# The second block's attention by pairs of heads, with the context's ahead and the convolution, pooling and output projections between the pairs

## What is computed

```python
h, hc = mod_norm(x, ...), mod_norm(xc, ...)
u = h @ w_in[l]
if last:  # second layer: of the context only keys and values
    kc, vc = heads(uc_kv[..., :NA_CH]), heads(uc_kv[..., NA_CH:])
else:
    yc = concatenate([gated_conv_mixer(...), multiscale_pool_mixer(...),
                      context_attention(heads(uc q), kc, vc)]) @ w_out[l]
    xc = xc + mc[:, 5, None] * yc
    xc = ffn_sublayer(xc, ...)
y = concatenate([gated_conv_mixer(...), multiscale_pool_mixer(...),
                 neighbourhood_attention(q, k, v, kc, vc, rpb[l])]) @ w_out[l]
x = x + m[:, 5, None] * y
```

## Time and profile before

| | us |
|---|---|
| median of 3 runs | 3614.18 (3612.76 to 3615.71) |
| the profiled execution | 3613.57 |
| its span in the profile | 3611.7 |

### The profile page before, as it was taken

One profiled execution on the slowest core, in us unless ns is written; L12 is line 12 of the kernel. 1 busy time (PEld: TensorE's weight loads), 2 busy tenths in 40 slices (PEclk: granted clock), 3 DMA queues, 4 the chain that ended last, 5 costly groups with the idle time before them and its releaser, 6 DMA issues.

```text
span 3611.7 us, 45968 instructions
## 1 busy us (share of the span) xinstructions
PE 3454.8 (96%) x18726; PEld 2954.7 (82%) x18726; DVE 1875.9 (52%) x3704; ACT 1145.2 (32%) x1886; POOL 275.4 (8%) x520
## 2 busy tenths in 40 slices
PE   6989899998999999999989999999999999999998
PEld 5778668886888888978878888888888888878886
DVE  5476678446555526356567774352222364653333
ACT  4465433224221224225432122242112242433222
POOL 0000011000111100301011110000000012100000
PEclk9999899999999999999999999999999999999999
DMA  4201245333434423410345553232122243123332
GB/s 125 91 24 43 74 136 179 99 100 112 130 125 129 118 72 115 123 47 13 94 152 159 158 161 108 85 103 65 59 65 65 76 135 108 33 60 98 94 99 76
DMA packets 381235, 352.57 MB, mean 98 GB/s; under 512 B 19440, under 2 KB 353136, under 8 KB 380640
## 3 DMA queue, kind: packets, MB, share of 16 engines
q1 hardware_dynamic: 348416, 255.47, 23.3%
q0 software_dynamic: 31168, 91.94, 8.4%
q10 hardware_dynamic: 1440, 2.22, 0.2%
HBM read 343.27 MB, written 2.10 MB: 96 GB/s over the span
## 4 chain that ended last, share of the span: by engine, by line
PE 85%; DVE 10%; ACT 4%; issue 1%; DMA 1%; ACTq 0%; DVEq 0%; POOLq 0%
PE ps L536 83%; PE ps L539 2%; DVE lob L1787 2%; DVE Tm L1899 1%; ACT hib L1178 1%; DVE Hl L1910 1%; DVE ACC L1876 1%; ACT Tm L1178 1%; ACT Hh L1178 1%; ACT L1178 0%; DVE HN L1919 0%; DVE MR L1807 0%; DVE Hl L1908 0%; DVE near_PTt L2435 0%; DVE C L1960 0%
## 5 line engine op out<-in xcount | busy, mean ns | idle before, releaser
L536 PE MATMUL ps<-Hh,hib 128*128 128x512 f32 (+1 forms) x3552 | 1260.7, 355 | 26.5 <-DVE lob L1787 16.8
L536 PE MATMUL ps<-Hl,hib 128*128 128x512 f32 (+1 forms) x3552 | 1253.1, 353 | 0.0
L536 PE MATMUL ps<-Hh,lob 128*128 128x512 f32 (+1 forms) x3552 | 1251.0, 352 | 0.0
L1787 DVE TENSOR_TENSOR lob<-rawb,hib 128x1024 fp32r<-128x1024 f32 (+2 forms) x487 | 582.9, 1199 | 1013.1 <-ACT hib L1178 1012.5
L1178 ACT ACTIVATE hib<-rawb 128x1024 fp32r<-128x1024 f32 (+2 forms) x487 | 501.1, 1033 | 1266.2 <-PE ps L536 1242.6
L536 PEld LDWEIGHTS ps<-Hh,hib 128*128 128x128 f32 x3552 | 677.9, 191 | 132.0 <-DVE lob L1787 19.8
L536 PEld LDWEIGHTS ps<-Hh,lob 128*128 128x128 f32 x3552 | 676.8, 191 | 91.1
L536 PEld LDWEIGHTS ps<-Hl,hib 128*128 128x128 f32 x3552 | 678.1, 191 | 89.3 <-issue 1.2
L536 PE MATMUL ps<-Gha,hib 128*128 128x512 f32 (+1 forms) x704 | 239.7, 340 | 6.6 <-DVE lob L1787 6.5
L536 PE MATMUL ps<-Gla,hib 128*128 128x512 f32 (+1 forms) x704 | 238.1, 338 | 0.0
L536 PE MATMUL ps<-Gha,lob 128*128 128x512 f32 (+1 forms) x704 | 238.1, 338 | 0.0
(11 more groups left out here) (254 smaller groups left out, 4018.1 us busy)
## 6 DMA issues: line engine op xcount, KB each, us to landing
rawb<-in_ffn_w_in SPq DMA_DIRECT2D x352, 256.0 KB, 3.3
rawb<-in_ffn_w_out SPq DMA_DIRECT2D x88, 512.0 KB, 3.4
MRb<-in_w_mod_t POOLq DMA_DIRECT2D x144, 256.0 KB, 3.4
rawb<-in_w_ff SPq DMA_DIRECT2D x64, 512.0 KB, 3.6
rawb<-in_w_in SPq DMA_DIRECT2D x62, 512.0 KB, 3.7
MRa<-in_w_mod_t POOLq DMA_DIRECT2D x96, 256.0 KB, 3.4
rawb<-in_ffn_w_out SPq DMA_DIRECT2D x44, 384.0 KB, 3.1
rawb<-in_w_out SPq DMA_DIRECT2D x28, 512.0 KB, 3.4
```

What stands on the lines that cost most here:

```text
L536: return e.matmul(out, lhsT, rhs, start=start, stop=stop)
L1787: e.tensor_tensor(lob_of(c), raw_of(c), hib_of(c), ALU.subtract).then_inc(*done(("lo", c.i)))
```

## The change

The chunks of `v2` have 512 columns. In layer 0 `conv`, `pool` and `q2` are swept for `c` alone first (12 chunks), then the context's attention runs, by pairs of heads (8 pairs), and `pool` and `conv` for `x` are swept tile by tile between those pairs; then the context's output projection, `q2` for `x`, and the attention of `x` (16 pairs) with the first half of its output projection (the four slices of convolution and pooling) between the first pairs. In layer 1 `q2` comes ahead of `conv` and `pool`, which lie between the pairs; the first half of the output projection starts behind the last scores. The queries of `x` go to the columns of `c` in `Hh` and `Hl`, so they need not wait until the sweeps of `x` are done. The second half of the output projection is last; in layer 0 the norm of `c` lies in it, and the norm of `x` lies between the first chunks of sublayer `b`. A pair is two heads of one block: PE makes both heads' scores, transposes and outputs in one step each, in the order transposes of p-2, scores of p, the work beside, outputs of p-2; DVE's order is scores of p, scaling of p-1, the work beside, final of p-3. What is left out of the diff: the same moves written for ACT, and functions of DVE that hold the old code under new names (`conv_stage`, `pooled`, `projected`, `mix_cp`, `half_residual`).

```diff
@@ -283,16 +283,38 @@
         ffn(("a", l), d["ffn_w_in_2"][l, 0], d["ffn_w_out_2"][l, 0], ["x", "c"], True)
         w = d["w_in_2"][l]
         for s, tiles in (("x", 4), ("c", 2)):
-            for half in range(2):
-                tm(("v2", l, s, half), w, 8, 2048 + 256 * half, 256, tiles)
+            tm(("v2", l, s), w, 8, 2048, 512, tiles)
         for pair in range(2):
             fm(("k2", l, pair), w, 8, [1536 + 256 * pair, 1664 + 256 * pair], ["x", "c"])
-        for stage, c0 in enumerate((0, 512, 256)):
-            fm(("conv", l, stage), w, 8, [c0, c0 + 128], full)
-        fm(("pool", l), w, 8, [768, 896], full)
-        for pair in range(2):
-            fm(("q2", l, pair), w, 8, [1024 + 256 * pair, 1152 + 256 * pair], full)
-        residual(("out2", l), d["w_out_2"][l], 8, full, l == 0)
+        def conv(s):
+            for stage, c0 in enumerate((0, 512, 256)):
+                fm(("conv", l, s, stage), w, 8, [c0, c0 + 128], [s])
+        def pool(s):
+            fm(("pool", l, s), w, 8, [768, 896], [s])
+        def queries(s):
+            for pair in range(2):
+                fm(("q2", l, s, pair), w, 8, [1024 + 256 * pair, 1152 + 256 * pair], [s])
+        if l == 0:
+            conv("c")
+            pool("c")
+            queries("c")
+            pool("x")
+            conv("x")
+            residual(("out2", l), d["w_out_2"][l], 8, ["c"], False)
+            queries("x")
+        else:
+            queries("x")
+            conv("x")
+            pool("x")
+        for half in range(2):
+            for pair in range(4):
+                name = (("out2", l, half), "x", pair)
+                P[name] = Sweep(name, [chunk(beside(d["w_out_2"][l][512 * half:512 * half + 512, 256 * pair:256 * pair + 256].rearrange(
+                    "(k p) n -> p k n", p=128)), 4 * half, 4, 256)], [(0, "x"), (1, "x")])
         ffn(("b", l), d["ffn_w_in_2"][l, 1], d["ffn_w_out_2"][l, 1], full, l == 0)
...
+def near_pairs(s):
+    return [(hp, j) for hp in range(4) for j in range(4 if s == "x" else 2)]
...
+def beside_pairs(l, s):
+    at = {n: [] for n in range(30)}
+    def put(step, *what):
+        at[step].append(what)
+    if (l, s) == (0, "c"):
+        put(1, "mix", "c")
+        for q in range(4):
+            put(q // 2, "tile", ("pool", l, "x"))
+            for stage in range(3):
+                put(2 + 2 * stage + q // 2, "tile", ("conv", l, "x", stage))
+        for n in range(2):
+            put(2 + n, "pooled", n)
+            put(4 + n, "project", n)
+            put(5 + n, "projected", n)
+        for stage in range(3):
+            put(4 + 2 * stage, "conv", stage)
+    elif l == 0:
+        put(0, "mix", "x")
+        for pair in range(4):
+            for n in range(2):
+                put(2 * pair + n + 1, "out", pair)
+            put(2 * pair + 3, "added", pair)
+    else:
+        for stage in range(3):
+            for q in range(4):
+                put((4 * stage + q) * 2 // 3, "tile", ("conv", l, "x", stage))
+            put((4 * stage + 3) * 2 // 3 + 1, "conv", stage)
+        for q in range(4):
+            put(8 + q // 2, "tile", ("pool", l, "x"))
+        for n in range(2):
+            put(10 + n, "pooled", n)
+            put(12 + n, "project", n)
+            put(13 + n, "projected", n)
+        put(15, "mix", "x")
+        for n in range(2):
+            put(17 + n, "out", 0)
+    return at
...
+def by_pairs(number, stages, skew, beside, beside_do):
+    for step in range(number + skew[-1]):
+        for f, late in zip(stages, skew):
+            if f == "beside":
+                for what, n in beside.get(step, []):
+                    beside_do(what, n)
+            elif f is not None and 0 <= step - late < number:
+                f(step - late)
...
+        def second_at(H_, k, s, j):
+            return query_at(H_, k, j) if s == "x" else H_[:, 4 + k, T + 128 * j:T + 128 * j + 128]
+        def made_at(H_, l, k, s, j):
+            return H_[:, 4 + k, 128 * j:128 * j + 128] if (l, s) == (0, "x") else second_at(H_, k, s, j)
+        def pool_buffer(l):
+            return near[l]["PTt"] if l == 0 else C[:, :, :].rearrange("p a b -> p (a b)")
+        def turned_keys(l, s, p, b):
+            return near[l]["PTt"][:, 512 * b:512 * b + 512] if s == "x" else near[l]["P"][:, 2 * (p % 2) + b, 256:512]
...
+                def n_scores(p_):
+                    hp, j = pairs[p_]
+                    w.wait_ge(*at("q2", l, s, hp))
...
+                    got = [take("s2", l, s, p_, b) for b in range(2)]
+                    for b, (bank, before) in enumerate(got):
+                        freed(before)
+                        if s == "x":
+                            w.wait_ge(*at("maskr", l))
+                            w.wait_ge(*at("identr"))
+                            mm(ps[:, bank, 0:256], identr[:, :], N["maskr"][:, 256 * KIND[j]:256 * KIND[j] + 256], True, False)
+                    for b in range(2):
+                        r = slice(64 * b, 64 * b + 64)
...
+                        if s == "x":
+                            bank = got[b][0]
+                            scores(ps[:, bank, 0:256].rearrange("p (i c) -> p i c", c=32), q_, near_keys, False)
+                            m = scores(ps[:, bank, 256:512], q_, context_keys, True)
+                        else:
+                            m = scores(ps[:, got[b][0], 0:TC], q_, context_keys, True)
+                    m.then_inc(*done(("scores2", l, s, p_)))
...
+                def n_turn(p_):
+                    n = 4 if s == "x" else 2
+                    got = [take("t2", l, s, p_, b) for b in range(2 if s == "x" else 1)]
+                    w.wait_ge(*at("scaled2", l, s, p_))
+                    for b in range(2):
+                        bank, before = got[b % len(got)]
+                        freed(before)
+                        for k in range(n):
+                            to = 128 * k + (0 if s == "x" else 256 * b)
+                            m = turn(ps[:, bank, to:to + 128], N["P"][:, 2 * (p_ % 2) + b, 128 * k:128 * k + 128])
+                    m.then_inc(*done(("turned2", l, s, p_)))
...
+                outs = [by_tile((("out2", l, 0), "x", pair), fm_products, mixed_acts(l), l == 0) for pair in range(4)]
+                by_pairs(len(pairs), [n_turn, n_scores, "beside", n_out, n_final], [2, 0, 0, 2, 3], beside_pairs(l, s), beside_do)
+                return outs
...
+            def project(l, s, n):
...
+                w.wait_ge(*at("pooled", l, s, n))
+                freed(before)
+                mm(ps[:, b, 0:nt], N["PW"][:, n, :], N["PV"][:, n, t0:t0 + nt], True, True).then_inc(*done(("pwfull", l, s, n)))
...
             def near_mixers(l):
                 acts = {"x": x_act(4 + 3 * l), "c": c_act(2 + 3 * l)}
                 for s in ("x", "c"):
+                    whole(("v2", l, s), tm_products, tm_act(acts[s]), cnorm(l, 1) if s == "x" else None)
+                    give_all(("v2", l, s))
                 for pair in range(2):
                     whole(("k2", l, pair), fm_products, acts)
                     give_all(("k2", l, pair))
+                if l == 0:
+                    for stage in range(3):
+                        whole(("conv", l, "c", stage), fm_products, acts)
+                        give_all(("conv", l, "c", stage))
+                    whole(("pool", l, "c"), fm_products, acts)
+                    give_all(("pool", l, "c"))
+                    for pair in range(2):
+                        whole(("q2", l, "c", pair), fm_products, acts)
+                        give_all(("q2", l, "c", pair))
+                    mark("pe", "hfree", "c", l)
+                    for n in range(2):
+                        project(l, "c", n)
+                        give("pw", l, "c", n)
+                    near_attention(l, "c")
+                    residual(("out2", l), ["c"], {"c": (Hh, Hl, T, TC, (lambda k: ("mix2", l, "c", k)), False)})
+                mark("pe", "cfree", l)
                 for pair in range(2):
+                    whole(("q2", l, "x", pair), fm_products, acts)
+                    give_all(("q2", l, "x", pair))
+                if l == 0:
+                    mark("pe", "hfree", "x", l)
+                outs = near_attention(l, "x")
+                for some in outs:
+                    for _ in some:
+                        pass
+                mark("pe", "qfree", l)
+                if l == 0:
+                    in_turn(grouped(norm_steps(*cnorm(l, 2)), NORM_BY_4))
+                residual(("out2", l, 1), ["x"], mixed_acts(l))
...
+                def n_turn(p_):
+                    w.wait_ge(*at("turned2", l, s, p_))
+                    if p_:
+                        w.wait_ge(*at("pout2", l, s, p_ - 1))
+                    elif s == "x":
+                        w.wait_ge(*at("pooled", 0, "x", 1) if l == 0 else (None, 0))
+                    if s == "x":
+                        for b in range(2):
```

(60 more changed lines are left out.)

598 lines of the change are left out of this document (294 added, 304 removed).

## The result

The change makes the kernel faster, where I forecast no gain: 3591.98 us (median of 4 runs, 3590.48 to 3599.08) against 3614.94 us (4 runs beside them), ratio 0.9939 (95% interval 0.9922 to 0.9957). The forecast was 3622 us, 3600 to 3640: wrong in its sign, and 8 us outside the range.

The account below looks back on a forecast made before the run. PE was taken as the bound. From the profiled 3613.57 us, 44.5 taken away and 47.2 added made +2.7, the clock +5.0: 3621.3, or 3622 us for the median, range 3600 to 3640.

Parts of the forecast that it names:

- The attention's switches: In both layers' attention a pair of x costs PE 4.91 us against 5.28 before; with c's pairs, -15.0 us.
- rival E: Last score of one head and first of the other overlap in all 40 pairs: -5, 3617 us; chance 0.07.
- small: Layer 1's halved slice multiplications +1.2 us, start 0.5, convolution bursts on DVE, banks and 24 switches to tiles 3.0.
- Pairs with nothing beside them: Attention steps without tiles: PE waits 1.3 us a pair for DVE's chain, 6.2 in all; layer 0 +11.0 us.
- Rival A: Pairs without tiles do not wait, DVE's chain taking under 2.3 us: 3601 us; chance 0.20.
- Starts: Start of c's attention: waits 1.8 and 2.3, +5.5 us; of x's in layer 0: waits 2.5 and 2.1, +6.5.
- Layer 1, steps 10 to 15: Two poolings of x on DVE under pairs without tiles: transposes wait 11.9 us, step 15 adds 2.0; +13.9 in all.
- Sweeps for c: Twelve chunks for c alone run at 2.9 us a chunk, cost 0; up to +8 us if loads lag.
- rival C: c's sweeps run at the pace of their loads, 0.7 us late in each of twelve: +8, 3630 us; chance 0.07.
- Layer 0's end: Behind layer 0 PE idles 17.2 us against 14.3, +2.9, and x's halves add 1.9: together +4.8 us.
- The clock: Half clock at pairs without tiles and layer 1's waits of 3.5 and 4.1 us: +5 us (0 to 14).
- rival B: Half clock lasts, three falls of 6 us each: 3632 us; sign: granted clock under 0.8 over tileless pairs; chance 0.15.

Follow-up runs that it names:

- pool_first: Changed kernel with layer 1's pooling sweep ahead of the convolution's, its two poolings in steps 2 and 3: 3589.36 us, ratio 0.9932 to the kernel before.
- heads_alternate: Changed kernel with the two heads' matmuls alternating, score by score and output by output: 3586.05 us, ratio 0.9931 to the kernel before.
- Scale_first: Changed kernel with DVE scaling the weights of pair p-1 before the scores of pair p: 3580.28 us, ratio 0.9912 to the kernel before.
- masks_apart: Changed kernel with each head's mask matmul directly ahead of its own six scores in pairs of x: 3619.26 us, ratio 1.0018 to the kernel before.

## Why the prediction was wrong, point by point

**The step that failed is "The attention's switches", its 4.91 us a pair, and with it rival E, which I priced at one score's 0.12 us.** Measured are 4.03. Not one score but three run beside the other head's, and four outputs do. Of the 0.88, 0.39 lie in the scores (1.25 for 1.64) and some 0.53 in the outputs (1.51 for 2.04). The steps with a tile, some 16 of the 32, save all of it, 14 us. In the others only the scores' part shortens the step, as the chain begins at the last score, and the outputs' part turned into wait (1.66 for my 1.3): the step is 5.75 us for 6.2, which saves 7. A pair of c costs 1.74 (outputs 0.60, transposes 0.58, scores 0.56) and not 2.56: both heads' scores, three each, run wholly side by side, and so do the outputs, four each; that is -6.5. Against it the tiles of a step cost 0.23 more than forecast (one 2.96 for 2.73, two 5.68 for 5.46), in 26 steps 6, of which 3.0 stood under "small": +3. Together -24 or -25 of the 26 us by which the profiled execution, its first part's 3.8 set aside, lies under my 3621.3. The median lies 30 us under my 3622, so some 5 are left; 3.4 of them, an estimate, are what the profiled execution took longer in layer 0 than two others of the same code, mostly by its clock (pool_first above).

**Why misled me.** I took eight outputs in a row in 1.12 us as two heads that don't overlap. They were four and four, and the second four had to wait for a copy on ACT. These are that stretch's weight loads and copy, from the trace of before:

```profile
1726.52 0.41 PEld L536 LDWEIGHTS ps<-near_PTt,near_VX 128*64 128x64 f32 x4 [0.17 <-issue]
...
1727.06 0.41 PEld L536 LDWEIGHTS ps<-near_PTt,near_VX 128*64 128x64 f32 x4
...
1726.62 0.38 ACT L1178 ACTIVATE near_PTt<-ps 128x256 f32<-128x256 f32 x1 [0.56 <-PE ps L539]
```

The copy ends at 1727.00, and the second four begin at 1727.06. The row joined two groups that were never free to overlap. With it I had argued the rival down to 0.07. The Trainium skill ("TensorEngine Tiling (Array Packing)", Key Properties), cited there for tiles that multiply in parallel, was right, and the runs agree: 16 outputs in 1.02 us in heads_alternate.

**Pairs with nothing beside them: right in mechanism.** Seven waits of 1.66 us for `near_P`, 5.75 us apart (forecast 1.3 and 6.2; 0.39 of the difference is the scores'). Scale_first and masks_apart move them as the chain says. Rival A is out.

**Starts.** C's: waits 2.1 and 2.0 against 1.8 and 2.3, right. X's in layer 0: 2.6 at the first output tile against 2.5, but the second, 2.1, did not come. Not foreseen: 2.5 us for `Hl` (L2681) at 1580 us. Layer 1 starts without a wait, as forecast.

**Layer 1, steps 10 to 15.** The transposes wait 1.66, 3.16, 2.18, 0.60, 1.66 and 0.65 us, and the outputs 1.54 more, together 11.5 against 13.9; half clock came there (a granted clock of 0.79 in the stretch above).

**Sweeps for c:** TensorE busy 35.09 of 35.09 us over the twelve chunks, 2.9 us a chunk at a DMA share of 0.50 and 151 GB/s, so no cost, and rival C is out. **Layer 0's end:** idle 7.6 + 8.1, 15.8 us against 17.2. The norm's DMA on POOL starts at 1799.07 and the wait ends 12.2 us later (12.0 forecast, before as in the earlier trace rows).

**The clock.** I added 5 us. From step 2 on layer 0's pairs ran at 1.00 (1668.77 to 1758.05 us), so rival B is out there. Some 3 us at half clock stood just ahead, behind the wait at the first output tile, and some 3.5 behind the wait at 1580 us. Layer 1's last pairs, with the waits, had 0.83 (3114.6 to 3165 us), not far above the 0.8 that I had named as B's sign, and layer 0's end 0.59. How these 5 split wasn't measured.

So the range was too narrow since it held the overlap at 5 us where it was worth some 27; all other terms together were within about 5 us, in part by luck, since some were too high (13.9 for 11.5 in layer 1, a wait of 2.1 that did not come) and others too low (a wait of 2.5 that I had not seen).

## What to carry to other kernels

Small matmuls of two heads that use different halves of the partitions, or write different halves of the columns, cost the time of one when they stand next to each other, best in turn (here twelve scores of two heads in 0.91 us, as six of one); a 128-partition matmul between them takes that away and costs a further change (0.75 us a pair here). A row that joins several instructions says nothing against overlap until what each waits for is known. And where a faster engine leaves itself longer waits, look at its clock before its gain is counted, and shorten the chain that it waits for in the same edit (0.9873 here, where the two edits alone gave 0.9931 and 0.9912).

## What the hardware showed that I had not expected

- In the changed kernel, where one head's matmuls all stand ahead of the other's, the second head's begin early: three scores and four outputs run beside the first head's last. By the records they start ahead of matmuls that precede them in the program (VB of head 2 at 1749.54, VX of head 1 still until 1749.9). The Trainium skill ("TensorE: Matmul & The Clock Gate", Part 3, What overlaps and what doesn't) says that matmuls start and end in program order, without reordering; these rows differ, and they decide here.
- A second change between 128 and 64 partitions within a pair cost 0.4 us. The rows of the kernel before had said so (0.37); I had taken 0.1 when I expected masks_apart.
- Useless matmuls in its waits took 5.6 us off layer 0's part of a kernel: the granted clock was 1.00 instead of 0.88 in one stretch, and 1.00 instead of 0.78 behind it.
